# SSD prompt part and gate spreads inside the odd projection's tiles; retention samples by column groups

## The reference

```python
def odd_mixer(h, pos, w_in, conv_w, conv_b, dt_bias, a_log, d_skip, ssd_norm, ret_norm, w_out, conv_buf, ssd_state, ret_state):
    z, xbc, dt, rq, rk, rv, rg = split_cols(h @ w_in, ODD_SIZES)
    ...
    xbc_act = jax.nn.silu(acc + conv_b.astype(f32))          # acc: causal convolution over 4 tokens
    ...
    yc, s_new = ssd_chunked(xs, dt, a, bm..., cm..., s0)
    yc = yc + d_skip.astype(f32)[:, None] * xs               # then gated by silu(z), rmsnorm in 2 groups
    ...
    yr, r_new = retention_chunked(rq, rk, rv, r0)            # then group_norm, gated by silu(rg)
    y = jnp.concatenate([yc, yr], axis=-1).astype(h.dtype) @ w_out

def ssd_chunked(x, dt, a, bm, cm, s0):                        # one step per chunk of 128 tokens
        cum = jnp.cumsum(dac, axis=-1)
        lmat = jnp.exp(jnp.where(causal, seg, -jnp.inf))      # seg = cum[t] - cum[s], 16 heads
        wmat = cb[:, :, None] * lmat * dtc[..., None, :]      # cb = C B^T, 2 groups
        y = einsum(wmat, xc) + jnp.exp(cum)[..., None] * einsum(cc, s)
        s = jnp.exp(cum[..., -1])[..., None, None] * s + einsum(w_end, bc, xc)
```

## Time and profile before

| | |
|---|---|
| median of 3 runs | 1963.99 us (1957.95 to 1972.39) |
| the profiled execution | 1960.23 us |
| its span, first to last instruction | 1958.4 us |
| PE busy | 1761.5 us (90%), 13456 instructions |
| DVE, ACT, POOL busy | 855.0, 610.2, 588.3 us |
| mean granted clock | 0.922 |
| chain that ended last | PE 77%, DVE 13%, ACT 3%, issue 3%, DMA 2% |

### The profile page before, as it was taken

The page is one execution under the profiler, slowest core; times in us unless marked ns, Lnnn a source line. Parts: engine busy times, 40 slices in busy tenths (PEclk is TensorE's granted clock), DMA queues, the critical chain, the costliest instruction groups (busy, mean ns, idle before and its releaser), DMA issues.

```text
span 1958.4 us, 31412 instructions
## 1 busy us (share of the span) xinstructions
PE 1761.5 (90%) x13456; PEld 1648.8 (84%) x13456; DVE 855.0 (44%) x1257; ACT 610.2 (31%) x1046; POOL 588.3 (30%) x260
## 2 busy tenths in 40 slices
PE   6999886987999999998999887866897899999998
PEld 5888555976999999998999856755786799999998
DVE  4775284624521112146947154659563452111211
ACT  3344203332432323232431211415333343232312
POOL 1322001430444444443543200002342144444442
PEclk9999567998999999999999976678999999999999
DMA  5221211370433333332332223114155033333332
GB/s 125 66 77 56 54 25 54 99 243 16 113 97 89 96 88 96 91 88 71 87 98 76 69 62 89 27 44 140 49 163 166 28 103 87 97 88 97 89 95 87
DMA packets 294588, 170.64 MB, mean 87 GB/s; under 512 B 18863, under 2 KB 281183, under 8 KB 294298
## 3 DMA queue, kind: packets, MB, share of 16 engines
q1 hardware_dynamic: 253016, 123.85, 22.8%
q10 hardware_dynamic: 41434, 44.79, 7.3%
HBM read 155.91 MB, written 13.84 MB: 87 GB/s over the span
## 4 chain that ended last, share of the span: by engine, by line
PE 77%; DVE 13%; ACT 3%; issue 3%; DMA 2%; ACTq 1%; POOL 0%; DVEq 0%; SPq 0%
PE banks L382 21%; PE banks L384 20%; PE banks L383 20%; PE banks L889 1%; PE banks L1824 1%; PE banks L732 1%; DVE norm_acc L312 1%; ACT w_hi L442 1%; PE banks L1849 1%; PE banks L2561 1%; PE banks L1865 1%; PE banks L2682 1%; PE banks L702 1%; DVE swa_s L1154 1%; PE banks L2641 1%
## 5 line engine op out<-in xcount | busy, mean ns | idle before, releaser
L453 POOL TENSOR_TENSOR w_lo<-w_raw,w_hi 128x1024 fp32r<-128x1024 f32 (+2 forms) x256 | 588.1, 2298 | 1353.1 <-ACT w_hi L442 1353.1
L382 PE MATMUL banks<-xn_hi,w_hi 128*128 128x260 f32 (+1 forms) x1920 | 552.4, 288 | 11.0 <-issue 7.2
L384 PE MATMUL banks<-xn_hi,w_lo 128*128 128x260 f32 (+1 forms) x1920 | 544.6, 284 | 0.0
L383 PE MATMUL banks<-xn_lo,w_hi 128*128 128x260 f32 (+1 forms) x1920 | 543.1, 283 | 0.0
L442 ACT ACTIVATE w_hi<-w_raw 128x1024 fp32r<-128x1024 f32 (+2 forms) x256 | 252.8, 988 | 859.9 <-PE banks L384 824.2
L382 PEld LDWEIGHTS banks<-xn_hi,w_hi 128*128 128x128 f32 (+1 forms) x1920 | 360.5, 188 | 17.5 <-issue 13.4
L383 PEld LDWEIGHTS banks<-xn_lo,w_hi 128*128 128x128 f32 (+1 forms) x1920 | 360.5, 188 | 1.3
L384 PEld LDWEIGHTS banks<-xn_hi,w_lo 128*128 128x128 f32 (+1 forms) x1920 | 360.4, 188 | 0.6
L382 PE MATMUL banks<-hid_hi,w_hi 128*128 128x260 f32 x1024 | 289.8, 283 | 0.0
L384 PE MATMUL banks<-hid_hi,w_lo 128*128 128x260 f32 x1024 | 289.4, 283 | 0.0
L383 PE MATMUL banks<-hid_lo,w_hi 128*128 128x260 f32 x1024 | 288.5, 282 | 0.0
(11 more groups left out here) (483 smaller groups left out, 2663.3 us busy)
## 6 DMA issues: line engine op xcount, KB each, us to landing
w_raw<-in_ffn_w SPq DMA_DIRECT2D x128, 512.0 KB, 4.1
w_raw<-in_odd_w_in SPq DMA_DIRECT2D x36, 512.0 KB, 3.8
kc<-in_cache_mem_k ACTq DMA_DIRECT2D x16, 512.0 KB, 8.4
vc<-in_cache_mem_v ACTq DMA_DIRECT2D x16, 512.0 KB, 7.6
w_raw<-in_even_w_in SPq DMA_DIRECT2D x14, 512.0 KB, 3.8
w_raw<-in_odd_w_out SPq DMA_DIRECT2D x24, 256.0 KB, 2.8
w_raw<-in_mem_wk SPq DMA_DIRECT2D x8, 512.0 KB, 3.9
w_raw<-in_mem_wq SPq DMA_DIRECT2D x8, 512.0 KB, 3.8
```

What stands on the lines that cost most here:

```text
L382: pe.matmul(out, hi[:, kk, 0:m], r, start=kk == 0, stop=False)
L383: pe.matmul(out, hi[:, kk, 0:m], q, start=False, stop=False)
L384: last = pe.matmul(out, lo[:, kk, 0:m], r, start=False, stop=kk == nk - 1)
L453: pool.tensor_tensor(k.w_lo[n % RING][:, view[0], view[1]], k.w_raw[n % RING][:, view[0], view[1]], k.w_hi[n % RING][:, view[0], view[1]]. ...
```

## The change

The SSD prompt part is no stage any more: `SsdPrompt` hangs its steps into the projection's tiles with `inside` and `follow`. Block n starts at tile t = 21 + 4n: exponents of two quarters ahead of part 0, turn of X ahead of part 5, the other quarters ahead of 6 and 7; in tile t+1 B and C (part 0), from block 1 the decays of head pairs 0 to 3 (part 1), state times C (3), decays of pairs 4 to 7 (6); in tile t+2 y (5) and the added state (6). VectorE's and ScalarE's steps follow tiles t-1 to t+2. The decays are spread per block, straight into `t`, from block 1 on; `RetPrompt` and `RetSample` spread none. All tiles of the projection use two pairs of banks, the rest use banks 4 to 7. The order of the tiles is dt, X B C, RQ RK, RV, RG, Z; the SiLU of RG and Z moves to ScalarE in `RetPrompt`; the exponential's table is loaded after tile 18. The gate spreads are put inside tiles 17 to 19. `ConvTurn` and `SsdTurn` become one `OddTurn` with six items, which stores the prompt's SSD state too and waits for it. `RetSample` lays the queries out with zeros between (`qz`), so that a product has 32 query columns as the stationary operand, the state as the moving one, and the four heads stand in four column groups; the result adds up over samples in one bank and is turned once. The samples' SSD states are loaded four by four, at the start of the retention's norm and of `SsdSample`, by ScalarE.

```diff
@@ odd_projection
+    order = [*range(O_X, O_X + 12), *range(O_RQ, O_RV), *range(O_RV, O_RG + 4), *range(O_Z, O_Z + 8)]
...
+    for t in tiles:
+        t["pairs"] = 2
+    follow(tiles, 18, None, lambda act, n: k.nc.scalar.preload_act_table_set("natural_log_exp_and_others"))
+    odd_spread(k, tiles, 17)
+    ssd = SsdPrompt(k, conv)
+    ssd.block_start(tiles, 21, 0)
     rope = Rope(k, [k.proj[:, c, :] for c in range(O_RQ, O_RV)], ODD, gates.rope_t)
     for j in range(8):
         i = 1 + order.index(O_RQ + j)
...
+        inside(tiles, i + 1, 4, lambda pe, j=j, n=len(k.tiles) + i: rope.pe_rotate(pe, j, k.tile_out, n + 1))
+        follow(tiles, i, lambda dve, n, j=j: rope.dve_apply(dve, j))
+    ssd.rope = rope
+    for n in range(NBLK):
+        if n:
+            ssd.block_start(tiles, 21 + 4 * n, n)
+        ssd.block(tiles, 21 + 4 * n, n)
@@ odd_spread
+    spread = Beside(k, 0, items, (4, 5))
+    for i in range(6):
+        inside(tiles, first + i // 2, 1 + 4 * (i % 2), lambda pe, i=i: spread.pe(pe, i))
+        follow(tiles, first + i // 2 - 1, lambda dve, n, i=i: spread.take(dve, i))
@@ RetPrompt.act
-        for i in range(4):
-            self.decays.take(act, i)
+        for c in (*range(O_RG, O_RG + 4), *range(O_Z, O_Z + 8)):
+            act.activation(k.proj[:, c, :], k.proj[:, c, :], ACT.Silu)
+        k.nc.scalar.preload_act_table_set("natural_log_exp_and_others")
@@ RetSample.pe_out
+        if b == 0:
+            pe.wait_ge(self.placed.s, 2)
         pe.wait_ge(self.r_new.s, b + 1)
         for h in range(4):
-            last = pe.matmul(k.ps[:, 0, 8 * h + b:8 * h + b + 1], k.ret_s[b // 4][:, b % 4, h, :],
-                             k.proj[:, O_RQ + h, SEQ + b:SEQ + b + 1], start=True, stop=True)
+            last = pe.matmul(k.ps[32 * h:32 * h + 32, 0, 0:P], self.qz[:, h, 32 * b:32 * b + 32],
+                             k.ret_s[b // 4][:, b % 4, h, :], start=b == 0, stop=b == 7)
@@ RetNorm.act
+        for b in range(4):
+            load_ssd(self.k, act, b)
+        super().act(act)
@@ SsdPrompt
+    def block_start(self, tiles, t, n):
+
+        for q in range(2):
+            inside(tiles, t, 0, lambda pe, q=q: self.pe_exponents(pe, n, q))
+            follow(tiles, t - 1, lambda dve, _, q=q: self.dve_mask(dve, n, q))
+        follow(tiles, t - 1, None, lambda act, _: self.act_exps(act, n, (0, 1)))
+
+    def block(self, tiles, t, n):
+
+        inside(tiles, t, 5, lambda pe: self.pe_x(pe, n))
+        follow(tiles, t - 1, lambda dve, _: self.dve_xdt(dve, n))
+        for q in (2, 3):
+            inside(tiles, t, 4 + q, lambda pe, q=q: self.pe_exponents(pe, n, q))
+            follow(tiles, t - 1, lambda dve, _, q=q: self.dve_mask(dve, n, q))
+        inside(tiles, t + 1, 0, lambda pe: self.pe_b_c(pe, n))
+        if n:
+            inside(tiles, t + 1, 1, lambda pe: self.pe_ec(pe, n, 0))
+            inside(tiles, t + 1, 3, lambda pe: self.pe_state(pe, n))
+            inside(tiles, t + 1, 6, lambda pe: self.pe_ec(pe, n, 1))
+            follow(tiles, t, None, lambda act, _: self.act_ec(act, n, 0))
+        follow(tiles, t, None, lambda act, _: self.act_b(act, n))
+        follow(tiles, t, None, lambda act, _: self.act_exps(act, n, (2, 3)))
+        if n:
+            follow(tiles, t, None, lambda act, _: self.act_ec(act, n, 1))
+            follow(tiles, t, lambda dve, _: self.dve_carried(dve, n))
+        follow(tiles, t + 1, lambda dve, _: self.dve_weights(dve, n))
+        inside(tiles, t + 2, 5, lambda pe: self.pe_y(pe, n))
+        inside(tiles, t + 2, 6, lambda pe: self.pe_added(pe, n))
+        follow(tiles, t + 2, lambda dve, _: self.dve_out(dve, n))
...
+    def pe_state(self, pe, n):
+        pe.wait_ge(self.masked.s, 4 * n + 4)
...
+    def pe_y(self, pe, n):
+        pe.wait_ge(self.w_ready.s, n + 1)
+        if n:
+            pe.wait_ge(self.y_scaled.s, n)
...
+    def dve_carried(self, dve, n):
+        dve.wait_ge(self.y_state.s, n)
+        dve.wait_ge(self.ec_ready.s, 2 * n)
+        for a in range(2):
+            t = self.t[:, 4 * a:4 * a + 4, :]
+            ins = dve.tensor_tensor(t, t, blocks(k.ps[:, 4 + a, :]), ALU.mult)
@@ odd_layer
-    s = [odd_projection(k, normed), ConvTurn(k), odd_spread(k)]
+    s = [odd_projection(k, normed), OddTurn(k)]
     s += [ret_turn(k), RetPrompt(k), RetSample(k), Center(k, "ret", [k.proj[:, O_RQ + h, :] for h in range(4)]),
-          ret_norm(k), SsdPrompt(k), SsdTurn(k), SsdSample(k), SsdNorm(k)]
+          ret_norm(k), SsdSample(k), SsdNorm(k)]
```

More of the change, by code:

```diff
@@ L2427, in ret_turn @@
     return Turn(k, "ret_turn", items)
-def spread_decays(k, which, pairs, banks):
-    return Beside(k, which, [(k.pair(j, 16, (0, SEQ), k.ecum[:, 0:SEQ]), lambda act, bank, j=j:
-                                                act.activation(k.ec[:, j, 0:SEQ], bank[:, :], ACT.Copy))
-                                               for j in pairs], banks)
 class RetPrompt(Stage):
@@ L2441, in __init__ @@
         super().__init__(k)
-        self.decays = spread_decays(k, 0, range(0, 4), range(4, 8))
         kept = k.mid.at
@@ L2529, in __init__ @@
         super().__init__(k)
-        self.decays = spread_decays(k, 1, range(4, 8), range(1, 4))
         k.small.reset(k.ret_kept)
         self.t = [k.small(f"rets_t{i}", [P, 4, P]) for i in range(2)]
+        k.mid.reset(8192)
+        self.qz, self.out = k.mid("rets_q", [P, 4, 256]), k.mid("rets_out", [P, P])
         self.vb, self.r_new, self.o = (k.counter(f"rets_{n}") for n in ("v_spread", "r_new", "o"))
+        self.placed, self.copied, self.turned = k.sample_signals
     def act(self, act):
         k = self.k
-        for i in range(4):
-            self.decays.take(act, i)
         for i in range(2):
@@ new lines, in pe_x, with pe_b_c @@
+        for j in range(8):
+            last = pe.transpose(ps[:, 6 + j // 4, (j % 4) * P:(j % 4) * P + P], p[:, O_X + j, c], k.c("ident"))
+        last.then_inc(self.xturn.s, 1)
+    def pe_b_c(self, pe, n):
+        k, ps, p, c = self.k, self.k.ps, self.k.proj, slice(n * P, n * P + P)
+        pe.wait_ge(self.xdt_ready.s, n + 1)
+        for g in range(2):
+            pe.transpose(ps[:, 6, g * P:g * P + P], p[:, O_B + g, c], k.c("ident"))
+        for g in range(2):
+            last = pe.matmul(ps[:, 6, (2 + g) * P:(3 + g) * P], p[:, O_B + g, c], p[:, O_C + g, c], start=True, stop=True)
+        last.then_inc(self.b_c.s, 1)
@@ new lines, in pe_ec @@
+    def pe_ec(self, pe, n, a):
+        k, c = self.k, slice(n * P, n * P + P)
+        if a:
+            pe.wait_ge(self.ec_ready.s, 2 * n - 1)
+        for j in range(4):
+            for (c0, c1), lhsT, rhs, row in k.pair(4 * a + j, 16, (j * P, j * P + P), k.ecum[:, c]):
+                last = pe.matmul(k.ps[row:row + 64, 7, c0:c1], lhsT, rhs, start=True, stop=True)
+        last.then_inc(self.spread.s, 1)
+    def pe_state(self, pe, n):
+        k = self.k
+        pe.wait_ge(self.masked.s, 4 * n + 4)
+        for j in range(8):
+            last = pe.matmul(k.ps[:, 4 + j // 4, (j % 4) * P:(j % 4) * P + P], k.ssd_state[:, 2 * j:2 * j + 2, :],
+                             k.proj[:, O_C + j // 4, n * P:n * P + P], start=True, stop=True)
+        last.then_inc(self.y_state.s, 1)
@@ new lines, in pe_y, with pe_added @@
+    def pe_y(self, pe, n):
+        k, ps = self.k, self.k.ps
+        pe.wait_ge(self.w_ready.s, n + 1)
+        if n:
+            pe.wait_ge(self.y_scaled.s, n)
+        for h in range(16):
+            j = h // 2
+            last = pe.matmul(ps[64 * (h % 2):64 * (h % 2) + 64, 4 + j // 4, (j % 4) * P:(j % 4) * P + P],
+                             self.xdt[n % 2][:, h, :], self.l[n % 2][:, h, :], start=True, stop=True)
+        last.then_inc(self.y.s, 1)
+    def pe_added(self, pe, n):
+        k = self.k
+        pe.wait_ge(self.bt_ready.s, n + 1)
+        if n:
+            pe.wait_ge(self.ec_ready.s, 2 * n)
+        for g in range(2):
+            last = pe.matmul(k.ps[:, 6 + g, :], self.bt[n % 2][:, g * P:g * P + P], self.xw[:, 8 * g:8 * g + 8, :],
+                             start=True, stop=True)
+        last.then_inc(self.added.s, 1)
@@ L2714, in dve_mask, with act_ec @@
+    def act_ec(self, act, n, a):
+        act.wait_ge(self.spread.s, 2 * n - 1 + a)
+        if a == 0:
+            act.wait_ge(self.state.s, n)
+        act.activation(self.t[:, 4 * a:4 * a + 4, :], blocks(self.k.ps[:, 7, :]), ACT.Copy).then_inc(self.ec_ready.s, 1)
     def dve_mask(self, dve, n, q):
@@ L2842, in act @@
     def act(self, act):
+        act.wait_ge(self.k.ssd_here.s, 64)
+        for b in range(4, 8):
+            load_ssd(self.k, act, b)
         prefetch_memory(self.k, act, self.mtok)
```

289 lines of the change are left out of this document (113 added, 176 removed).

## The result

The changed kernel takes 1934.5 us (median of 4 runs, 1929.7 to 1938.8) against 1963.1 for the kernel before (4 runs), a ratio of 0.985 with a 95% interval of 0.981 to 0.988. Profiled, the span is 1927.9 us instead of 1958.4, 30.5 less, where the forecast was 23 less and 1937 for the profiled execution; the execution profiled is the fastest of the four, so the 28.6 between the medians is the better measure.

What follows compares the result with a forecast made beforehand. TensorE was taken as what the kernel waits for in its weight products, with partly idle stages between. 112.9 us go and 89.7 come: 23 less, 1937 profiled, 1941 beside the median 1964; range 1915 to 1962.

Steps and rivals of the forecast that it cites:

- (a): SSD prompt stage and its turn, from the norm's end to the first sample product: 91.2 us go away.
- (b): The stage that spreads the gates: 5.2 us go away.
- (d): Retention samples: column groups and no decay spreads make them 16.3 us instead of 31.4, 15.1 gone.
- (c): Retention prompt part: loses the eight spreads of decays, blocks 4.4 to 4.5 us instead of 4.8, 1.4 gone.
- Inserted products and passages: Projection tiles: blocks 47.1, gate spreads 2.7, switches between product kinds 5.5; together 55.3 us come in, not hidden.
- Waits: Projection tiles 21 to 36: TensorE waits before y and before the next exponents, 18.8 us, bounds 0 and 40.
- xw's place: Tile t+1: xw comes after w_lo began and is held by it, so TensorE waits 3.65 us before y.
- The rival: Projection: w_lo doesn't hold VectorE's instructions, or they come first; waits 9.8 us instead of 18.8, kernel 1925; chance 0.25.
- The clock: Projection: slow weight products after each of three waits of 3.65 lose 2.1 us, 6.3 in all; waits of 2.75 cost nothing.
- The slower rival: Tiles 21 to 36: TensorE at half clock for long stretches; 80 us of it would give 1981; chance 0.08.
- VectorE's end: After the projection's last tile VectorE ends 3.5 us after TensorE against 2.0 before: 1.5 more.
- The turn: Odd layer's turn: six items copied and p_ssd must land before the stage ends, 3.8 us more, from 2.3 to 7.

Runs made afterwards that it cites:

- the first experiment: Changed kernel with a memset of 384 columns of xw ahead of the multiply that writes xw, blocks 1 to 3; stretch 178.9 us against 163.0.
- the four orders: Changed kernel with state update before multiply-adds, two ScalarE queue orders changed, y and added state in their tile's last part; 1918.3 us, ratio 0.977.

## Why the prediction was right, and where it was not

The direction and the size hold (23 less forecast, 28.6 as medians), but several terms were off and partly made up for each other.

- **What goes.** (a) and (b), 96.4, were read from windows and are gone. (d) 15.8 instead of 15.1. (c) 0.6 instead of 1.4: from the stage's first product to the samples' first it was 23.4 and is 22.8. A block bound by VectorE's state update takes 4.6 us, not 4.4 to 4.5, and TensorE now waits 1.05 for VectorE in the first block, where the spread used to stand; that wait the forecast put at nothing.
- **Inserted products and passages.** Forecast 55.3. The groups' net times on TensorE's timeline sum to 53.7 for the four blocks, and tiles 17 to 20 are 4.2 longer (w_lo starts 9.0, 7.6 and 7.5 us apart instead of 6.6): 57.9. The passage was priced at 0.09 each way for all groups; it is 0.39 in and out together for the exponents' groups of 16 rows (0.19 behind a wait) and nothing for the state's, the added state's and most transposes, whose neighbours have 128 rows as they do.
- **Waits.** Forecast 18.8, measured 10.4. The step that failed is xw's place: "due at V+1.5, starts at V+3.6", V being the end of tile t+1. It was due at V+1.07 (the tile ended at 1085.3, xw started at 1086.35), because TensorE took 1.65 from the second decay spread to the tile's end, not 1.45, and VectorE's multiply was done 0.4 after that end; w_lo came at V+1.2 as forecast, and the order was turned round. The rival named this ("xw is only 0.35 us too late to come before POOL"). The multiply-adds were held, as forecast, and cost 2.4 instead of 2.75. With xw late the wait is 3.51: the mechanism was right, the place in time was not.
- **The clock.** Forecast 6.3, behind the three waits before y. In fact 13.7 us stood at 0.5, and cost 5.9: 163.0 less 153.0 (128 rows, no half clock, the same waits) are 10.0, of which 9 x 0.39 + 3 x 0.19 = 4.1 are the passages. The sum is near by luck, for its reason was wrong: no stretch followed a wait before y, two followed the waits of 2.4 that were charged with nothing, and with more rows none follows those either. The slower rival had the cause in hand ("16 rows in 3.7 of 9.0 us"), at a sixth of the 80 us at half pace that it would have needed for 1981. The only stretches away from the exponents came at the waits of 3.5 us in the first experiment, which were not there in the changed kernel; whether they would come without 16-row products in the stream was not run. In the Trainium skill, TensorE: Matmul & The Clock Gate, section HAM oscillation, the gaps that pay the slow clock each time are waits of some 3 to 5 us; the prediction read the rule as holding for its five waits above 2 us. The three of 3.5 agree with the section; seven gaps of 0.94 to 2.44 brought nothing once the rows were 128.
- **The projection's end and what follows.** 1.5 was forecast for VectorE's end; it is nothing (1.8 us from the last product to the turn, 2.1 before). The last block's eight multiply-adds are not held: the w_lo of that tile has 512 columns, takes 1.29 and ends just before them. The turn has 4.1 more (3.8 forecast), the norm 5.2 (4.0): 4.25 of it are the four issues, the rest a slower clock in its products.

Sum by these: -96.4 - 15.8 - 0.6 + 75.2 - 0.4 + 4.1 + 5.2 = -28.7 of the 30.5. The other 1.8 lie in stages that the change doesn't touch and that differ as much from run to run. Of the projection's 75.2, 57.9 + 10.4 + 5.9 = 74.2 are accounted for; 0.6 more is lost in its first tile at half clock, 0.4 stays open.

## What to carry to other kernels

Where products are put into a dense stream, look at their rows as well as at their time: the spread of 16 rows cost up to 0.39 us more per group and brought stretches at half the clock, and rows of zeros in a tile that was there anyway took both away (the ratio to the kernel before went from 0.985 to 0.979 in the changed kernel and from 0.977 to 0.971 beside the four orders). When VectorE and POOL meet at nearly the same moment, work out which comes first to a few tenths of a us, since the one behind is held until the other is nearly or quite done (0.96 us for w_lo behind xw, 1.83 for xw behind w_lo). And an experiment that removes a wait and finds the clock better has not shown that the wait alone was the reason: here zero rows removed every stretch with the waits left in, and two executions of one kernel differed by 7 us at half pace.

## What the runs showed of the hardware that was not expected

- **Rows and clock.** In nine profiled executions with exponents of 16 rows the clock stood at 0.5 for 3.4 to 34.1 us of these tiles, with idle times from 0 (none over 0.4) to 17.4 us; in four with 64 or 128 rows for 0. All the stretches with 16 rows but the three at the waits of 3.5 us began during the exponents or within 1 us of a group's end. Six of the thirteen executions ran on one chip: 20.5, 10.2 and 6.8 us with 16 rows, 0 three times with 128. Zeros in the added rows did as well as other data. That this holds for products of 16 rows at every share of the stream isn't shown: the spreads of the gates (tiles 17 to 20) and the decays' spreads have 16 rows too, stayed as they were, and brought no stretch in those four.
- **Passage.** A group of exponents with 16 or 64 rows between weight products takes 0.39 us more than the same group with 128 rows (0.19 behind a wait). The Trainium skill, TensorEngine Tiling (Array Packing), section Key Properties, says that changing the tiling mode of the array drains it. The numbers fit that, but no row of the trace names a mode or a drain, so it isn't shown that this is the reason.
- **The shared port.** xw first by 0.1 us: w_lo 3.36 us instead of 2.40; w_lo first by 0.4 us: xw 3.05 instead of 1.22. The Trainium skill, SBUF — State Buffer, section Who interferes with whom, says that an instruction of VectorE with two SBUF inputs contends with GpSimd's reads, and that the order of issue decides who blocks; both orders are in these traces and agree.
